# Narrow projections on 32-column strips, norm vectors folded into the weights, and a reordered last group in a three-block transformer kernel

## What is computed

```python
def rmsnorm(x, g):
    y = xf * lax.rsqrt(jnp.mean(xf * xf, axis=-1, keepdims=True) + EPS)
    return y.astype(x.dtype) * g
# GLA layer: h = rmsnorm(x, g_mix[0]); q, k, v, r, alr (16 columns), mq = split(h @ w_in)
#            log_a = log_sigmoid(alr @ w_alpha + b_alpha) / 16
# NSA layer:
kv = (rmsnorm(x, g_kv) @ w_kv)            # k and v of the three branches, 768 columns
k_cmp = gelu(blocks(k_c) @ w_ck1) @ w_ck2 # and the same for v: 31 blocks of 32 tokens, 2048 -> 256 -> 64
h = rmsnorm(x, g_mix[1])
q, gl, mq = split(h @ w_in)               # 512, 24 and 512 columns; gates = sigmoid(gl)
# mixed layer: proj = rmsnorm(x, w) @ w_mix_in, with 8 narrow columns (ga, gb) among the rest
```

## Time and profile before

| | |
|---|---|
| median of 3 runs | 2054.99 us (2054.3 to 2055.11) |
| profiled execution | 2054.38 us, its span 2052.7 us |
| TensorE matmul busy | 1967.0 us, 96% of the span |
| VectorE, ScalarE, GpSimd busy | 1121.0, 738.0, 182.7 us |
| DMA moved | 167.69 MB, mean 82 GB/s |

### The profile page before, as it was taken

The page is one execution under the profiler, slowest core; times in us unless marked ns, Lnnn a source line. Parts: engine busy times, 40 slices in busy tenths (PEclk is TensorE's granted clock), DMA queues, the critical chain, the costliest instruction groups (busy, mean ns, idle before and its releaser), DMA issues. The chain is left out here.

```text
span 2052.7 us, 27271 instructions
## 1 busy us (share of the span) xinstructions
PE 1967.0 (96%) x10497; PEld 1604.5 (78%) x10497; DVE 1121.0 (55%) x1616; ACT 738.0 (36%) x1145; POOL 182.7 (9%) x178
## 2 busy tenths in 40 slices
PE   7999999999999898889999999999988999999998
PEld 7888688888788875568888878788777688888786
DVE  6435456556535536636565553648555467777532
ACT  7442542222324426524222232424543342222333
POOL 2201020000002004402000000200141020000001
PEclk9999999999999998999999999999999999999999
DMA  6311132332333510023333323232010132322321
GB/s 232 117 48 42 58 92 88 107 97 91 99 97 86 145 53 1 1 72 92 103 92 97 97 93 99 74 95 83 11 43 2 62 92 83 113 91 90 105 82 41
DMA packets 135400, 167.69 MB, mean 82 GB/s; under 512 B 28307, under 2 KB 102536, under 8 KB 135304
## 3 DMA queue, kind: packets, MB, share of 16 engines
q1 hardware_dynamic: 135123, 166.32, 26.1%
q10 hardware_dynamic: 180, 0.05, 0.0%
HBM read 164.24 MB, written 2.10 MB: 81 GB/s over the span
## 5 line engine op out<-in xcount | busy, mean ns | idle before, releaser
L178 PE MATMUL bank<-h_hi,w_hi 128*128 128x512 f32 x2192 | 860.9, 393 | 23.7 <-DVE h_lo L406 6.8
L179 PE MATMUL bank<-h_lo,w_hi 128*128 128x512 f32 x2192 | 856.2, 391 | 0.0
L180 PE MATMUL bank<-h_hi,w_lo 128*128 128x512 f32 x2192 | 855.6, 390 | 0.0
L142 DVE TENSOR_TENSOR w_lo<-raw,w_hi 128x1024 fp32r<-128x1024 f32 x290 | 356.8, 1246 | 622.2 <-ACT w_hi L136 621.7
L136 ACT CAST w_hi<-raw 128x1024 fp32r<-128x1024 f32 x290 | 300.7, 1047 | 638.8 <-PE bank L178 629.0
L178 PEld LDWEIGHTS bank<-h_hi,w_hi 128*128 128x128 f32 x2192 | 413.2, 189 | 117.5 <-issue 11.5
L179 PEld LDWEIGHTS bank<-h_lo,w_hi 128*128 128x128 f32 x2192 | 413.4, 189 | 86.6 <-issue 1.4
L180 PEld LDWEIGHTS bank<-h_hi,w_lo 128*128 128x128 f32 x2192 | 413.3, 189 | 86.5
L1484 ACT ACTIVATE scratch<-scratch 128x512 f32<-128x512 f32 x66 | 41.8, 633 | 250.1 <-DVE scratch L1548 250.1
L306 POOL TENSOR_TENSOR tail<-keep 128x512 f32<-128x512 f32 x7 | 9.7, 1383 | 1239.2 <-ACT keep L290 1221.9
L1547 DVE SCALAR_TENSOR_TENSOR scratch<-keep,vecs,scratch 128x512 f32<-128x512 f32 x88 | 66.1, 752 | 10.2 <-DVE scratch L1546 1.1
(11 more groups left out here) (477 smaller groups left out, 1910.4 us busy)
## 6 DMA issues: line engine op xcount, KB each, us to landing
raw<-in_w_up SPq DMA_DIRECT2D x176, 256.0 KB, 3.1
raw<-in_w_down SPq DMA_DIRECT2D x44, 512.0 KB, 3.2
raw<-in_w_ffn_up SPq DMA_DIRECT2D x88, 256.0 KB, 3.3
raw<-in_w_mix_in SPq DMA_DIRECT2D x24, 512.0 KB, 3.8
raw<-in_w_ffn_down SPq DMA_DIRECT2D x22, 512.0 KB, 3.4
raw<-in_w_mem_kv SPq DMA_DIRECT2D x16, 512.0 KB, 4.8
raw<-in_a_w_in SPq DMA_DIRECT2D x16, 512.0 KB, 3.7
raw<-in_a_w_out SPq DMA_DIRECT2D x8, 512.0 KB, 4.8
```

What stands on the lines that cost most here:

```text
L142: dve.tensor_tensor(k.w_lo[n % RING][:, :], k.raw[n % RING][:, :], k.w_hi[n % RING][:, :].bitcast(F32), ALU.subtract)\
L178: a = pe.matmul(out, sh, mh, start=first, stop=False)
L179: pe.matmul(out, sh, ml, start=False, stop=False)
L180: c = pe.matmul(out, sl, mh, start=False, stop=last)
```

## The change

1. **Residual rounded once for both norms of the NSA layer.** The feed-forward stage before it now rounds x itself (`unit_gain`), and `stage_nsa_in` no longer rounds h a second time. The norm vectors g_kv and g_mix[1] go into the split of 8 weight chunks each (`weights_gained`: 0 to 7 and 16 to 23), which is then made of two halves with a vector each.
2. **Narrow tiles on strips.** `pe_few_columns` replaces `pe_few` in three stages: float32 matmuls of a 32-column weight (norm vector multiplied in by VectorE) against `xT`, number kk writing to PSUM partitions 32j to 32j+31, j = kk mod 4. The four partial sums are added where the tile is used next: by `k.fold`, a 128 x 32 matrix of four stacked identities, in place of the transposes (NSA gates, mixed layer), or by w_alpha loaded four times (GLA).
3. **Compressed keys and gates inside the last group** of `stage_nsa_in`: they are its `aside` before the third chunk; the gates no longer stand behind the group. ScalarE's order changes with it.
4. In the mixed layer the 8 VectorE operations that scale `xT` for the final norm move behind the narrow tile, since that now reads `xT`.

```diff
 def split_hi(k, act, upto):
     while k.ring.hi_at < min(upto, k.phase_end):
-        split_hi_chunk(k, act, k.ring.hi_at)
+        n = k.ring.hi_at
+        if n in k.chunk_gain:
+            split_hi_gained(k, act, n, lambda n, i: k.vec(k.chunk_gain[n] + i))
+            continue
+        split_hi_chunk(k, act, n)
         k.ring.hi_at += 1
...
+def weights_gained(k, name, n, groups):
+    for c in range(4 * groups):
+        k.chunk_gain[n + c] = VEC_ROWS[name] + 2 * (c % 4)
...
-def pe_few(k, pe, t, weights):
+def pe_few_columns(k, pe, t, w):
     if t >= 8:
         pe.wait_ge(k.tile_free.sem, k.tile_free.at(t - 7))
     for kk in range(8):
-        _, mm = pe_three(k, pe, bank(k, t)[:, :], [w[:, kk, :] for w in weights],
-                         (k.h_hi[:, kk, :], k.h_lo[:, kk, :]), kk == 0, kk == 7)
+        j = kk % 4
+        mm = pe.matmul(bank(k, t)[32 * j:32 * j + 32, :], w[:, kk, :], k.xT[:, kk, :], start=(kk < 4), stop=(kk >= 4))
     mm.then_inc(k.tile_full.sem, 1)
... stage_gla_in
             sp.dma_start(w_alr[:, :, :], a["a_w_in"][0].rearrange("(k p) n -> p k n", p=P)[:, :, 1536:1552]).then_inc(alr_in, 16)
-            sp.dma_start(w_alpha[0:16, :], a["a_w_alpha"][0]).then_inc(w_in, 16)
+            sp.wait_ge(ones_row, 1)
+            for j in range(4):
+                sp.dma_start(w_alpha[32 * j:32 * j + 16, :], a["a_w_alpha"][0]).then_inc(w_in, 16)
...
-            scaled(4, k.alrT[0:16, :])
+            for j in range(4):
+                r = slice(32 * j, 32 * j + 16)
+                ins = dve.tensor_tensor(k.alrT[r, :], bank(k, 4)[r, :], k.rstd[r, :], ALU.mult)
... stage_nsa_in, VectorE
-            split_lo(k, dve, first + 12)
-            for half in range(2):
-                for kk in range(4 * half, 4 * half + 4):
-                    dve.wait_ge(k.h_rounded.sem, k.h_rounded.at(8 + kk + 1))
-                    dve.scalar_tensor_tensor(k.h_lo[:, kk, :], k.xT[:, kk, :], g_mix(kk), k.h_hi[:, kk, :].bitcast(F32),
-                                             ALU.mult, ALU.subtract).then_inc(k.h_ready.sem, 1)
-                split_lo(k, dve, first + 14 + 2 * half)
-            small(2)
+            split_lo(k, dve, first + 17)
+            dve.tensor_tensor(wg_gained[:, :, 0:24], wg, g_row.unsqueeze(2).broadcast_to([P, 8, 24]), ALU.mult).then_inc(small_lo, 1)
             split_lo(k, dve, first + 23)
... stage_nsa_in, ScalarE
             read_out(6, 4)
-            split_hi(k, act, first + 12)
-            act.wait_ge(k.ring.used, first + 8)
-            for half in range(2):
-                for kk in range(4 * half, 4 * half + 4):
-                    act.activation(k.h_hi[:, kk, :], k.xT[:, kk, :], ACT.Copy, scale=g_mix(kk)).then_inc(k.h_rounded.sem, 1)
-                split_hi(k, act, first + 14 + 2 * half)
-            act.wait_ge(k.ring.used, first + 12)
-            small(2)
-            read_out(10, 2)
+            split_hi(k, act, first + 15)
+            read_out(10, 1)
+            split_hi(k, act, first + 19)
+            read_out(11, 1)
             split_hi(k, act, first + 23)
             read_out(16, 2)
-            read_out(19, 2)
+            split_hi(k, act, first + 24)
+            read_out(19, 3)
             split_hi(k, act, first + 28)
-            read_out(25, 1)
... stage_nsa_in, TensorE: the compressed keys and values, and
+                for tt in range(4):
+                    mm = pe.matmul(bank(k, t + 2)[:, tt * 24:(tt + 1) * 24], gates_t[:, tt * P:(tt + 1) * P], k.fold[:, 0:24],
+                                   start=True, stop=True)
+            pe_group(k, pe, t + 3, [feature_tile(k, m * P) for m in range(4)], aside=(2, compressed_and_gates))
             pe_used(k, pe)
-            pe.wait_ge(k.tile_free.sem, k.tile_free.at(19))
-            for tt in range(4):
-                mm = pe.transpose(bank(k, t)[:, tt * 24:(tt + 1) * 24], gates_t[0:24, tt * P:(tt + 1) * P], k.ident[0:24, 0:24])
```

More of the change, by code:

```diff
@@ L925, in _ @@
                     pe.wait_ge(k.tile_free.sem, k.tile_free.at(t + c // 2 - 7))
-                mm = pe.matmul(bank(k, t + c // 2)[:, (c % 2) * 256:(c % 2) * 256 + 256], k.alrT[0:17, c * P:(c + 1) * P],
-                               w_alpha[0:17, :], start=True, stop=True)
+                mm = pe.matmul(bank(k, t + c // 2)[:, (c % 2) * 256:(c % 2) * 256 + 256], k.alrT[:, c * P:(c + 1) * P],
+                               w_alpha, start=True, stop=True)
                 if c % 2:
@@ L1366, in stage_ffn @@
     UP, TOTAL = 4 * GROUPS, 4 * GROUPS + FT
+    if next_weights is not None:
+        weights_gained(k, next_weights, first + TOTAL, 2)
     down0 = first + UP
@@ L1704, in _ @@
             dve_sums(k, dve, now, (6, 7))
-            dve_next(k, dve, now, g_kv, range(4, 8))
+            dve_next(k, dve, now, unit_gain, range(4, 8))
             split_lo(k, dve, first + 7)
@@ L1760, in _ @@
         def _(act):
-            act_next(k, act, now, g_kv, range(4, 8), (6, 7))
+            act_next(k, act, now, unit_gain, range(4, 8), (6, 7))
             split_hi(k, act, first + 4)
```

134 lines of the change are left out of this document (69 added, 65 removed).

## The result

The changed kernel took 2040.8 us (median of 4 runs, 2038.7 to 2042.8) beside 2054.6 us for the kernel before on the same chip (4 runs, 2053.1 to 2055.1): a ratio of 0.9934, 95% interval 0.9922 to 0.9945. That is 13.8 us less; forecast were 2038.5 us and a range of 2036 to 2043. So in the two traces the difference is 11.7 us.

The account below looks back on a forecast made before the run. TensorE, busy 96% of the span, was taken as the bound. Gains of 3.5 + 2.8 + 7.2 + 0.9 + 0.7 + 1.4 = 16.5 us from 2054.4 gave 2037.9, with 0.6 to the median 2038.5 us; range 2036 to 2043.

Parts of the forecast that it names:

- Narrow tiles: GLA and mixed layer: four strips run at once, 2.0 us a tile instead of 5.5, 3.5 us gained in each.
- in pairs: Rival: only two strips run at once, tile 3.6 us, 1.6 lost in GLA and mixed layer each; 2041.7 us, chance 0.12.
- in turn: Rival: strips run one after another, tile 6.9 us; kernel 2051 us, chance 0.05.
- Nothing overlaps on strips: Rival: each strip switch waits for a drain and a load, tile 12.5 us; kernel 2068 us, chance 0.02.
- The fold: Mixed layer: four transposes become four float32 matmuls, 0.95 us against about 0.3, 0.7 us lost.
- Hidden layers to query group: stage_nsa_in: query group starts at 706.0 instead of 713.24, 7.2 us gained, plus 0.9 from the clock.
- The links of the load: Hidden layers: chunk 16's load issued at 697.7, landing at 702.4 to 703, split ready at 705.4 to 706.
- Query group to last group: stage_nsa_in: last group ends as if begun 2.6 us earlier, less 1.9 for the aside; net gain 0.7 us.
- the end: End of stage_nsa_in: one table load instead of two, pause 3.1 us instead of 4.5, gain 1.4 us.
- a sign of being wrong: Last group of stage_nsa_in: a clock of 0.5 after the wait for gelu would show the forecast wrong.
- main case: Whole kernel: all steps as summed, 2038.5 us, own range 2036.3 to 2040.5, chance 0.67.
- late loads: Rival: loads limit the hidden layers, chunk 16 ready only at 709.5 and the clock drops; 2043 us, chance 0.09.

Follow-up runs that it names:

- experiment 2: Changed kernel with each strip's two narrow matmuls directly after one another (strips 0,0,1,1,2,2,3,3): 2041.3 us, 0.9935 of the kernel before.
- experiment 3: Changed kernel with the narrow matmuls on strips 0,1,0,1,2,3,2,3: 2040.9 us, 0.9928 of the kernel before.
- Experiment 5: Kernel before with only the first three query chunks' splits moved ahead of the second hidden tile's read-out, h still rounded twice: 2049.7 us, 0.998.
- experiment 6: Changed kernel with both hidden-tile read-outs on ScalarE put back ahead of all query chunks' splits: 2043.4 us, 0.9952 of the kernel before.
- Experiment 7: Changed kernel with the compressed keys ahead of the last group and the gates' transposes behind it: 2045.9 us, 0.9966 of the kernel before.
- experiment 4: Kernel before with narrow tiles on strips in GLA and the mixed layer only, attention stage as it was: 2050.1 us, 0.9981.
- experiment 8: Five unread matmuls in the delta stage's 4.8 us pause: added to the changed kernel 2035.3 us, 0.9903; added to the kernel before 2052.1 us, 0.9995.

## Why the prediction was right

**Narrow tiles.** Forecast was 2.0 us a tile between the bounds of 1.7 and 6.9, and 3.5 us gained in each of two stages. Measured 1.92 us, and pieces shorter by 3.9 and 3.4 us. The step from two strips, which the trace of before showed, to four was right; the rivals "in pairs" and "in turn" fall by the first row of the tile, and experiments 2 and 3 add that not even a program in that order brings them about. "Nothing overlaps on strips" falls with them. The Trainium skill ("TensorEngine Tiling", Theoretical Speedup) gives up to 4x here: by the distance of 0.43 us in turn, 16 records would take 6.9 us, and 6.9 / 1.92 = 3.6. The 2.38x of "TensorE: Matmul & The Clock Gate" (Measured speedup vs the span model) is for three strips, which no run here has. A drain on changing the tiling mode ("TensorEngine Tiling", Key Properties) costs next to nothing here: the strips begin 0.88 us after the first of the eight narrow matmuls ahead of them, where the old tile began after 0.82, and the next group begins 0.5 us after the last strip record, where the distance within a strip is 0.43.

**The fold.** Forecast 0.7 us lost, measured 0.6 in the piece from the fold to the norms. VectorE's eight operations cost nothing, as forecast:

```profile
1347.10 5.38 DVE L2352 SCALAR_TENSOR_TENSOR xT<-xT,vecs,tail 128x512 f32<-128x512 f32 x8
1352.40 1.22 DVE L142 TENSOR_TENSOR w_lo<-raw,w_hi 128x1024 fp32r<-128x1024 f32 x1
1356.19 1.23 DVE L142 TENSOR_TENSOR w_lo<-raw,w_hi 128x1024 fp32r<-128x1024 f32 x1 [2.57 <-ACT w_hi L136]
```

The split behind them is late, the one after it waits for ScalarE again for 2.57 us: the slack has swallowed it.

**Hidden layers to query group.** Forecast: the query group starts 12.4 us after the first hidden matmul (706.0 against 693.6). Measured: 12.1 (703.30 against 691.17). The links of the load held: eight chunks 11.8 us (11.6), first query chunk landed 9.3 us after the start (8.8 to 9.4), ready 2.8 us after that. As forecast, the load is the last link, as ScalarE's 1.32 us for it shows; TensorE waits 0.35 us for it. Forecast gain 7.2 + 0.9 for the clock = 8.1, measured 8.3 in the piece from the first hidden matmul to the transposes. That the two are so near is partly luck. The prediction read 713.24 as the start of the old query group, and it was 712.43. So the group starts 18.8 us after the first hidden matmul before and 12.1 after, a gain of 6.7 and not 7.2. The group itself shrinks from 23.5 to 21.9 us, 1.6 for the clock and not 0.9. The two errors cancel. The first term also holds clock: the hidden layers of before lost 1.7 us to it, which the prediction did not name there. Experiment 5 shows that 5.9 us come from the order of ScalarE's and VectorE's queues alone, 3.2 of them by the clock; experiment 6 shows the 4.4 us that this order is worth once the rest is done, 1.7 of them by the clock. The prediction priced the rounding and the order together and didn't part them.

**Query group to last group, and the end.** Forecast 0.7 + 1.4 = 2.1 us, measured 2.1. The wait in the first chunk was to be 1.5 us; it is 0.29 for VectorE's read-out and 1.25 for gelu. The pause at the end is 3.1 us as forecast. Experiment 7, without the clock's 3.0 us, gives 1.0 and 1.4 us for the two steps. But experiment 2 shows that the clock can fall behind this wait of 1.3 us. The prediction named this as a sign of being wrong, without a price for it; it would have been 1.7 us.

**What failed.** Sum of the steps: 16.5 forecast, 17.1 measured. The forecast was 2038.5 us, the result 2040.8. That is inside the stated range but 0.3 us outside the main case's own range of 2036.3 to 2040.5. The upper part of the stated range was there for strips in pairs and late loads, and neither came about; that it also held what did come about is luck. That was a term which the prediction put at nothing without naming it: that untouched stages stay as long as they were. The products of the delta stage grew by 2.9 us because TensorE was granted the lower clock for longer behind a pause that both kernels have. Experiments 4, 5 and 8 show that it goes with the edit that puts the tiles of GLA and the mixed layer on strips, not with `stage_nsa_in`, and that it is the clock: all eight runs with those strips have 63.8 to 64.1 us unless the pause is filled, the three runs of the old tiles without the filling 61.2. Of the rest, 1.1 and 1.0 us in two long pieces, the first is a granted clock that differs between two runs of the same kernel; the second wasn't taken apart, and it is 552.4 to 554.2 us in the runs with the same program there.

Open stays why one and the same pause is answered by 1.7 us of low clock in one kernel and by 3.4 in the other, with 1.7 more behind the next pause. What the traces show is when the clock falls: 23.9 to 24.0 us behind the first product in the three runs of the old tiles, 0.2 to 0.3 us before TensorE resumes, and then it is low for 3.4 us; 23.2 to 23.5 us in the eight with strips, 0.7 to 1.1 us before TensorE resumes, and then it is low for 6.8 us. What TensorE did in the 22 us from the first product is alike to 0.04 us of busy time, and in the filled kernels 42.4 us of all engines are alike, so it must be something further back. That it is the strips themselves, and not merely where a change moves the fall of the clock against the program, isn't shown; no experiment here parts the two.

## What to carry over

Ask of an operation in an engine's queue not what it costs but what stands behind it: three splits moved ahead of one read-out won 5.9 us in their piece (2.7 of waiting, 3.2 of clock) and 3.9 in the whole kernel, where the strips won 6.7 in two stages and 3.6 in the whole. On TensorE a narrow output of up to 32 columns can go to four strips of the array, 1.9 us for eight 128x512 float32 products, if the four partial sums can be folded by a matmul that is needed anyway. And count a pause of TensorE with what the clock may take behind it: here nothing to 3.4 us a pause, 1.7 once behind a wait of only 1.3 us. Compare the stages that a change doesn't touch too, since it can shift these losses. Where nothing can be moved into a pause, a few matmuls whose result nothing reads gave 4.3 us back in one kernel and nothing in the other, so they must be measured in the kernel at hand.

## What the runs showed of the hardware

Four strips of 32 columns run at once in each of the three orders tried: 1.92 us in rounds, 1.94 in turn, 1.94 in pairs. A weight load of 128x32 float32 takes 106 to 110 ns, one of 128x128 190. The granted clock of a stretch does not follow from the pause ahead of it alone: behind 4.8 us it was low for 1.7 us' worth in one kernel and 3.4 in the other, behind 2.4 us it was 1.00 before, 0.72 over 6 us after, 0.62 and 0.52 in before with the first pause filled, and 1.00 in after with it filled, although 42.4 us ahead of it were alike in the last two. Behind a wait of 1.3 us it was 1.00 in the changed kernel and 0.55 over 3.8 us in the run of experiment 2.
